# Feed-forward of a hybrid encoder block: token block sums taken from turned tiles, and half of their low parts moved to POOL

## The reference, cut to what matters

```
        h = rms_norm(x, norm_ffn_pre[l])
        gate, up = jnp.split(h @ ffn_w_gu[l], 2, axis=-1)
        f = (jax.nn.silu(gate) * up) @ ffn_w_down[l]
        x = x + rms_norm(f, norm_ffn_post[l])
```

## Time and profile before

| what | us |
|---|---|
| median of 3 runs | 1398.59 (1397.63 to 1400.22) |
| the profiled execution | 1398.22 |
| its span | 1396.1 |
| PE busy | 1373.2 (98%) |
| DVE, ACT, POOL busy | 883.2, 669.1, 876.7 |

### The profile page before, as it was taken

How to read it: one execution, slowest core, us unless ns; L and a number is a source line. 1 busy time by engine, 2 the same in 40 slices (tenths; PEclk the granted TensorE clock), 3 DMA queues, 4 the chain that set the end, 5 groups by cost and what they waited for, 6 DMA issues and landing times.

```text
span 1396.1 us, 18962 instructions
## 1 busy us (share of the span) xinstructions
PE 1373.2 (98%) x6708; PEld 1142.7 (82%) x6708; DVE 883.2 (63%) x1262; ACT 669.1 (48%) x1357; POOL 876.7 (63%) x604
## 2 busy tenths in 40 slices
PE   8999999999999999999999999999999999999998
PEld 7998888756988888888888888888888888888886
DVE  5799997887987788764277533333333333484868
ACT  6432233666686774354374533333333333544454
POOL 1697256422778976512354687777777774799653
PEclk9999999999999999999999999999999999999999
DMA  5676133440028554301535132333332324933364
GB/s 203 210 248 210 46 91 105 152 151 1 1 61 282 188 190 148 101 28 39 188 118 187 58 109 98 111 113 114 98 108 99 111 83 166 364 110 96 112 206 154
DMA packets 137757, 183.58 MB, mean 131 GB/s; under 512 B 10304, under 2 KB 82368, under 8 KB 137664
## 3 DMA queue, kind: packets, MB, share of 16 engines
q1 hardware_dynamic: 135360, 177.25, 38.8%
q10 hardware_dynamic: 2304, 5.13, 1.1%
HBM read 136.98 MB, written 45.35 MB: 131 GB/s over the span
## 4 chain that ended last, share of the span: by engine, by line
PE 78%; POOL 7%; DVE 6%; ACT 3%; issue 3%; DMA 3%; SPq 0%; DVEq 0%; POOLq 0%; ACTq 0%
PE ps L1368 23%; PE ps L1369 23%; PE ps L1370 23%; PE ps L1359 4%; PE ps L1882 2%; PE ps L1542 1%; POOL wd L1329 1%; PE ps L1580 1%; POOL w_lo L1231 1%; DMA gain_b<-f_rows 1%; PE ps L1634 1%; POOL right_b L1320 1%; DVE x L3774 1%; POOL right_a L1320 1%; POOL ws L1277 1%
## 5 line engine op out<-in xcount | busy, mean ns | idle before, releaser
L1368 PE MATMUL ps<-w_hi,t_hi 128*128 128x512 f32 (+2 forms) x576 | 219.5, 381 | 2.5 <-DVE t_lo L2990 0.7
L1370 PE MATMUL ps<-w_hi,t_lo 128*128 128x512 f32 (+2 forms) x576 | 217.5, 378 | 0.0
L1369 PE MATMUL ps<-w_lo,t_hi 128*128 128x512 f32 (+2 forms) x576 | 217.5, 378 | 0.0
L1123 POOL TENSOR_TENSOR w_lo<-raw,w_hi 128x512 fp32r<-128x512 f32 (+1 forms) x52 | 82.1, 1585 | 96.5 <-ACT w_hi L2161 96.3
L1368 PEld LDWEIGHTS ps<-w_hi,t_hi 128*128 128x128 f32 x576 | 108.2, 188 | 21.9 <-issue 1.7
L1370 PEld LDWEIGHTS ps<-w_hi,t_lo 128*128 128x128 f32 x576 | 108.2, 188 | 17.6
L1369 PEld LDWEIGHTS ps<-w_lo,t_hi 128*128 128x128 f32 x576 | 108.2, 188 | 16.9
L1247 POOL TENSOR_TENSOR w_lo<-raw,w_hi 128x512 fp32r<-128x512 f32 x32 | 41.9, 1314 | 98.3 <-ACT w_hi L2638 98.2
L3667 DVE TENSOR_TENSOR ev<-ps,ev 128x512 f32<-128x512 f32 x21 | 14.5, 692 | 138.2 <-PE ps L1370 138.2
L2161 ACT ACTIVATE w_hi<-raw 128x512 fp32r<-128x512 f32 (+1 forms) x52 | 31.4, 615 | 96.5 <-PE ps L1370 96.1
L2837 ACT ACTIVATE ev<-ps 128x512 f32<-128x512 f32 x63 | 37.5, 595 | 83.7 <-PE ps L1370 83.7
(11 more groups left out here) (390 smaller groups left out, 4144.4 us busy)
## 6 DMA issues: line engine op xcount, KB each, us to landing
raw_a<-in_ffn_w_gu_dram SPq DMA_DIRECT2D x44, 256.0 KB, 3.2
raw_b<-in_ffn_w_gu_dram SPq DMA_DIRECT2D x44, 256.0 KB, 3.2
f_rows<-fs SPq DMA_DIRECT2D x44, 256.0 KB, 3.8
gain_b<-f_rows SPq DMA_DIRECT2D x39, 256.0 KB, 2.7
tables<-f_rows SPq DMA_DIRECT2D x38, 256.0 KB, 2.7
f_rows<-fa SPq DMA_DIRECT2D x33, 256.0 KB, 3.4
raw<-in_xa_wo_dram SPq DMA_DIRECT2D x32, 256.0 KB, 2.6
wd_rest<-in_ffn_w_down_dram SPq DMA_DIRECT2D x15, 512.0 KB, 6.3
```

The costliest lines, as they stand in the source:

```text
L1123: nc.gpsimd.tensor_tensor(w_lo[:, k, 0:width], raw[:, k, 0:width], w_hi[:, k, 0:width].bitcast(F32), ALU.subtract).then_inc(w_split, 1)
L1368: nc.tensor.matmul(out, a_hi, b_hi, start=start, stop=False, skip_group_check=onto)
L1369: nc.tensor.matmul(out, a_hi, b_lo, start=False, stop=False, skip_group_check=onto)
L1370: return nc.tensor.matmul(out, a_lo, b_hi, start=False, stop=stop, skip_group_check=onto)
```

## The change

The token sums are now formed from tiles that have been turned already, and no sum is turned.

- `row_high(t)` for t < 4 copies each bank raw into `y[:, t, ...]` (the turned tile, kept in fp32) ahead of its high part: eight more ACT copies of 128x512. `xo_round(31)` now stands ahead of `row_high(3)`.
- `sum_rows_12(m)` reads the turned tile 4+m straight from its PSUM bank, so PE turns tiles 6 and 7 only when `sum_rows_12(0)` and `(1)` have let go of their banks. PE turns one tile after each of the products 0 to 3 of chunk 0.
- `third_sums(p)` and `fourth_sums(p)` (both DVE) do two tiles each, 128x1024. POOL's four `fourth_rows` are gone.
- `sum_high(n)` and the low parts do two tiles at once: 8 of 128x1024 in place of 16 of 128x512. Low parts 0 to 3 (first and second sum) are on DVE, low parts 4 to 7 (third and fourth) on POOL (`late_sum_low`).
- The weights of chunk 1 are split in the order `SUMS_AHEAD` (2, 3, 4, 5, 0, 1, 6), and two `weight_sum_of(2, n)` come between the late low parts.

```diff
 def row_high(t):
                     act.wait_ge(h_turned, 2 * t + half + 1)
+                    if t < 4:
+                        nc.scalar.activation(y[:, t, half * 512:(half + 1) * 512], bank(4 + 2 * (t % 2) + half),
+                                             ACT.Copy).then_inc(h_raw, 1)
...
 def turn_rows_h3(t):
+                    if t >= 6:
+                        pe.wait_ge(t_rows, 2 * (t - 6) + half + 1)
...
 def sum_high(n):
+                if n < 2:
+                    act.wait_ge(t_rows, 4 * n + 4)
...
+                if n == 2:
+                    act.wait_ge(g_prod, 6)
                 elif n == 4:
-                    act.wait_ge(g_prod, 6)
-                elif n == 8:
-                    act.wait_ge(t_rows, 12)
-                    act.wait_ge(t_rows4, 4)
-                act.wait_ge(t_turned, T_TURNED + n + 1)
-                nc.scalar.activation(sum_home(n)[0], four(6 + n % 2), ACT.Copy).then_inc(t_high, 1)
+                    act.wait_ge(t_rows, 10)
+                    act.wait_ge(t_rows4, 2)
+                    act.wait_ge(t_low, 4)
+                elif n == 6:
+                    act.wait_ge(t_low, 6)
+                nc.scalar.activation(sum_home(n)[0], turned_sums(n), ACT.Copy).then_inc(t_high, 1)
...
 # POOL
-            fourth_rows(0) ... fourth_rows(3)
+            for j in SUMS_AHEAD:
                 weight_low(1, j)
+            def late_sum_low(n):
+
+                pool.wait_ge(t_high, T_HIGH + n + 1)
+                high, low = sum_home(n)
+                nc.gpsimd.tensor_tensor(low, turned_sums(n), high.bitcast(F32), ALU.subtract).then_inc(t_low, 1)
+
+            late_sum_low(4)
+            late_sum_low(5)
+            late_sum_low(6)
+            weight_sum_of(2, 1)
+            late_sum_low(7)
+            weight_sum_of(2, 2)
...
 # PE
-            for n in range(3):
+            for n in range(4):
                 first_chunk(n)
                 turn_rows_h3(4 + n)
...
-            for j in range(6):
-                turn_sums((4 + 2 * j, 5 + 2 * j))
-                block_product(1, j)
...
 # ACT, from row_high(5) on
+            first_silu(0)
+            row_high(6)
+            weight_high(1, 2)
+            weight_high(1, 3)
+            row_high(7)
+            sum_high(0)
+            weight_high(1, 4)
+            weight_high(1, 5)
+            sum_high(1)
+            weight_high(1, 0)
+            sum_high(2)
+            sum_high(3)
+            weight_high(1, 1)
+            weight_high(1, 6)
+            first_silu(1)
+            bank_copy(1, 1)
+            weight_high(2, 0)
+            sum_high(4)
+            sum_high(5)
...
 # DVE
             row_low(4)
+            sum_rows_12(0)
             row_low(5)
+            sum_rows_12(1)
             row_low(6)
             row_low(7)
+            sum_rows_12(2)
+            sum_rows_12(3)
...
             first_gated(0)
             sum_low(0)
             sum_low(1)
-            sum_rows_3(0)
-            sum_rows_3(1)
+            third_sums(0)
+            third_sums(1)
             sum_low(2)
+            fourth_sums(0)
             sum_low(3)
+            fourth_sums(1)
             first_gated(1)
```

More of the change, by code:

```diff
@@ L92, in c_weights, with c_weight @@
     return 4 + PROD * (c - 1) + n if c else n
+SUMS_AHEAD = (2, 3, 4, 5, 0, 1, 6)
+def c_weight(c, j):
+    return c_weights(c, (SUMS_AHEAD.index(j) if c == 1 else j) + 1)
 def c_sums(c, n=0):
@@ L691, in sum_rows, with turned_sums @@
             kind, m = n // 4, n % 4
-            return (y[:, 4 + m, 512:1024], y[:, 4 + m, 0:512], y[:, m, 0:512], t_sum[:, m, :])[kind]
+            return (y[:, 4 + m, 512:1024], y[:, 4 + m, 0:512])[kind]
         def sum_home(n):
-            kind, m = n // 4, n % 4
+            kind, m = n // 2, n % 2 * 2
             high, low = tok_sums[(2, 1, 3, 4)[kind]]
-            c = slice(m * P, (m + 1) * P)
-            return high[:, :, c], low[:, :, c]
+            c = slice(m * P, (m + 2) * P)
+            return tuple(v[:, :, c].rearrange("p k (m i) -> p m k i", m=2) for v in (high, low))
+        def turned_sums(n):
+            kind, m = n // 2, n % 2 * 2
+            v = (y[:, 4 + m:6 + m, 512:1024], y[:, 4 + m:6 + m, 0:512], y[:, m:m + 2, 0:512], t_sum[:, m:m + 2, :])[kind]
+            return v.rearrange("p m (k i) -> p m k i", k=4)
         def memory_slots(n):
@@ L1294, in _ @@
                 weight_sum_of(1, n)
[L1295 to L1300, removed]
-                weight_low(1, j)
+            for j in SUMS_AHEAD:
+                weight_low(1, j)
+            def late_sum_low(n):
[8 more added lines that the diff above has]
+            weight_sum_of(2, 2)
             for c in range(2, NC):
                 weight_low(c, 0)
-                weight_sum_of(c, 1)
+                if c > 2:
+                    weight_sum_of(c, 1)
                 weight_low(c, 1)
-                weight_sum_of(c, 2)
+                if c > 2:
+                    weight_sum_of(c, 2)
                 weight_low(c, 2)
@@ L1990, in first_chunk @@
                 last.then_inc(g_prod, 1)
[L1992 to L2006, removed]
             def block_product(c, j):
@@ L2032, in block_product @@
                 last.then_inc(g_prod, 1)
-            for n in range(3):
+            for n in range(4):
                 first_chunk(n)
                 turn_rows_h3(4 + n)
-            turn_rows_h3(7)
-            first_chunk(3)
             first_chunk(4)
[L2040 to L2044, removed]
-            for j in range(6):
-                turn_sums((4 + 2 * j, 5 + 2 * j))
-                block_product(1, j)
-            block_product(1, 6)
-            for c in range(2, NC):
+            for n in range(5, 8):
+                first_chunk(n)
+            for c in range(1, NC):
                 for j in range(PROD):
@@ L2785, in _ @@
             row_high(2)
-            for n in range(26, 31):
+            for n in range(26, 32):
                 xo_round(n)
             row_high(3)
-            xo_round(31)
             for t in range(4, NT):
@@ L2807, in _ @@
             row_high(5)
[L2809 to L2829, removed]
             def bank_copy(c, n):
@@ L2837, in bank_copy, with first_silu @@
                 nc.scalar.activation(dst, bank(3 * (c % 2) + src_bank), ACT.Copy).then_inc(c_act, 1)
+            def first_silu(n):
+                act.wait_ge(g_prod, (2, 7)[n])
+                nc.scalar.activation(gate[:, n, :], bank(2 * n), ACT.Silu).then_inc(c_act, 1)
+            first_silu(0)
[17 more added lines that the diff above has]
+            sum_high(5)
             def gate_silu(c, n):
@@ L2844, in _ @@
             for c in range(1, NC - 1):
[L2845 to L2849, removed]
+                if c > 1:
+                    bank_copy(c, 1)
+                    weight_high(c + 1, 0)
                 weight_high(c + 1, 1)
@@ L2852, in _ @@
                 if c == 1:
-                    sum_high(12)
-                    sum_high(13)
+                    sum_high(6)
+                    sum_high(7)
                 if c > 1:
```

69 lines of the change are left out of this document (31 added, 38 removed).

## The result

Before 1398.91 us (median of 10 runs, 1397.49 to 1400.22), after 1402.74 (10 runs, 1400.55 to 1405.22): ratio 1.0028, 95% interval 1.0019 to 1.0037. The change costs 3.8 us. The profiled execution took 1403.47, its span is 1401.3.

What follows compares the result with a forecast made beforehand. PE bounds the kernel, already held by ACT and POOL at (2, 5). Gains of 7.0 + 0.4 less losses of 0.5, 1.2, 0.6, 0.2, 1.3, 4.6 and about 2.0 net +3.0: median 1401.6 us, range 1397.6 to 1404.2.

Steps and rivals of the forecast that it cites:

- What PE saves: Eight pairs of `turn_sums` leave PE at 0.88 us each, 7.0; with 0.44 for the old wait at (2, 5), some 7.5.
- Step 1: Raw copies while tiles 0 to 3 are turned delay POOL's low parts; PE loses 0.5 us, bounds 0 and 1.0.
- Step 2: Turning tiles 6 and 7: no wait at tile 6; PE waits 1.2 us for the low part of tile 7.
- Step 3: DVE's list to the fourth token sum: three meetings with POOL cost 3.1 us, so it is done at 779.0.
- Step 4: POOL's list, late low parts at 2.36 us: chunk 2's fourth weight sum ends at 802.95, 3.0 late.
- Step 5: PE waits 0.6, 0.2 and 1.3 us in chunk 1, 4.6 at (2, 2); (2, 5) starts 3.0 later.
- about 2.0, the last to (2, 5): PE loses about 2.0 us at (2, 5), waiting for `bank_copy(2, 4)`.
- rival D: The 4.6 us pause at (2, 2) lowers PE's clock; time within C's 1403 to 1405; chance no more than 0.03.
- All is shifted by the same from there: Behind (2, 5) POOL gains on PE in each chunk as before, and everything is later by the same 3.0 us.
- A, faster: Rival: gain holds if chunk 2's fourth weight sum ends before 799.96 less POOL's catch-up; 3.6 us faster, 1395.0; chance 0.10.
- B: As a rival: a tie, some 1399, if DVE loses nothing to POOL or step 1 is hidden; chance 0.27.
- C: Rival: low parts take up to 3.4 us or DVE loses 1.3 per POOL operation; 1403 to 1405; chance 0.13.

Runs made afterwards that it cites:

- e3: Changed kernel with 38 transposes of the identity added on PE ahead of its wait at (2, 2); median 1402.29 us, ratio 1.003 to the kernel before.
- e7: Kernel before, with none of the change, `weight_low(2, 0)` done three times on POOL; median 1401.26 us, ratio 1.0018 to the kernel before.
- e4: Changed kernel with late low parts 4 and 5 on DVE, 6 and 7 on POOL behind two weight sums; median 1399.42 us, ratio 1.0006 to the kernel before.
- e2: Changed kernel with `gate_silu(1, 1)` and `bank_copy(2, 1)` ahead of `weight_high(2, 4)` and `(2, 5)` on ACT; 1403.36 us, ratio 1.0034 to the kernel before.
- e8: Changed kernel with POOL waiting for the fourth token sum ahead of `weight_low(1, 1)`; measured once, 1402.19 us.
- e5: Changed kernel with all late low parts on DVE and product 3 of chunk 0 cut around tile 7's turn; 1394.82 us, ratio 0.9967 to the kernel before.

## Why the prediction was right

Forecast 1401.6 with +3.0; measured 1402.74, +3.8 in the medians, inside the range of 1397.6 to 1404.2 and slower by 0.28%. By its own steps:

- **What PE saves.** 7.0 for eight pairs isn't seen alone, but the account closes with it: with the old wait, 0.6 by starts, it is 7.6; less what PE lost by its starts (0.5 in step 1, then 1.2, 0.5, 0.3, 1.3, 4.65 and 2.9, all below) that is -3.8, and (2, 5) starts 4.51 later than in the earlier trace rows, 3.8 with the later start of this profile taken off (709.83 against 709.13).
- **Step 1.** Predicted 0.5; from the turn of tile 0 to that of tile 4 40.52 in place of 40.00.
- **Step 2.** Tile 6: no wait predicted and none found; the 0.2 for `t_lo` in the list of waits stands at the turn of tile 2, at 717.43, and was there before too (716.73). Tile 7: 1.2 predicted; from its turn at 761.19 to product 4 at 763.20 are 2.01, where 0.79 pass from the turn of tile 6 to its product, so 1.2 found.
- **Step 3.** The fourth token sum at 779.0; at 779.36, in a trace that is 0.7 late by then. Three DVE operations took 1.1 more than their 1.2, 3.3 in all where 3.1 was taken: one of the two of 3.46, and those of 2.30 and 2.31. POOL's 1.30 became 2.3 in two of these three meetings. The Trainium skill ("SBUF — State Buffer", "Who interferes with whom") calls the shared ports an exclusive lock. The trace agrees, and shows why the price is 1.1 and not the 1.3 that POOL's operation takes alone: the one that comes later waits for what is left of the other. At 772.55 POOL had 1.23 to go and DVE lost 1.1; at 773.74 DVE had 1.11 to go and POOL lost 1.0; at 774.78 POOL had 1.23 to go and DVE lost 1.1.
- **Step 4.** The fourth weight sum at 802.95; at 803.35, that is 2.7 late and not 3.0 with the later start taken off. The operation not in the trace, the late low part, took 2.37 to 2.39 (4.76 for two): the value taken, 2.36, and not the 3.4 of the upper bound.
- **Step 5.** Predicted 0.6, 0.2, 1.3 and 4.6 at (1, 4), (1, 5), (1, 6) and (2, 2). By starts (to the matmul ahead, less one step of 0.23) 0.50, 0.27, 1.29 and 4.65. The row's own figure for a wait is 0.16 less, since it counts from the end of the matmul ahead (0.39 after its start), while the next would have started 0.23 after it.
- **The term that was mis-sized, and its mechanism wrong,** is the last: "about 2.0, the last to (2, 5)", as a wait. PE never waited there. It ran 14 steps in 6.11 us (805.68 to 811.79) where 3.2 would do, 2.9 lost, and came to (2, 5) at 816.82, when the bank copy of 814.90 had been done for 1.3. With the clock kept full (e3) the term is sound: PE waits 1.8 there by starts. So rival D, given 0.03, was what happened at that place. The 0.9 between 2.9 and 2.0 is why (2, 5) comes 3.8 later and not 3.0. D's argument, "PE stood 5.17 us at the start and its clock was still granted in full", was a wrong reading: the twelve transposes behind that pause took 2.82 us, where sixteen took 1.91 in the earlier trace rows and 38 of the same identity 4.31 in e3, so PE ran there at about half speed. The views print a full clock for that stretch, but the trace holds no clock record ahead of 9.71 us. That the medians say 3.8 too is in part luck, since B adds 0.8 in the profile.
- **All is shifted by the same from there.** Nearly: B is 0.8 longer, where e7, with POOL as late, has none of it (561.84). In it stands a wait of 1.50 in the down projection, in the row below this list, where the earlier trace rows have 0.5 for POOL. No releaser is named for it, but POOL's `right_b` ends at 1245.42. Further back ACT stands 2.22 at 1209.94 for the load of a left part (`gain_b` from `f_rows`), where the seven loads ahead of it cost 0.86 to 1.48. The other kernels made from the changed one have 1.0 to 1.4 at that place of PE (e4 0.35 and 0.47), e7 0.16 and 0.44. What makes the load late in them wasn't tried and stays open.
- **The rivals.** A, faster: shown to be reachable, but not with the late low parts on POOL. "If it ends before 799.96" was the right place: with that sum at 794.86 the kernel is 5.0 faster by the medians, at 800.05 it is even, at 803.35 slower. B and C: DVE's three meetings came as counted, so neither.

The wait in the down projection, from PE's timeline of the changed kernel:

```profile
1245.52 0.47 PE L1387 MATMUL ps<-right_b,left_b 128*128 128x512 f32 x1 [1.50 <-issue]
```

## What to carry to other kernels

Work taken off the bounding engine is worth only what its suppliers can follow. Before counting the gain, look for the place where that engine already waits a little, and follow its releaser back: the 0.44 us at (2, 5) told more than the 7 us saved.

Where an operation goes to another engine, ask what is behind it in that list and who waits for the last item, and when its own input can be there: four operations on POOL cost 7.2 us of its list, two placed behind a late input still 4.7, and the same four on DVE a wait of 0.15 of PE at (1, 4).

An interval on the bounding engine's timeline ranks kernels well: A lay within a microsecond of what the medians said in each comparison made here.

## What the runs showed of the hardware

PE's granted clock fell to half, 1.2 GHz, with pauses inside a busy stretch: 4.49 us in the changed kernel, 4.17 in e2, 4.39 in e8 and 3.27 in e4 (granted clock 0.72 over 800 to 806 us). It was back in full some 6 us after the restart in the changed kernel and in e2, and 3.3 us after it in e4. It stayed full behind waits of 1.65 (e3), 1.63 (e7), 1.46 (e8) and 1.24 (e2). But a pause of 2.04 was enough once, in e5's execution, far ahead of the change:

```profile
444.82 0.47 PE L1383 MATMUL ps<-w_hi,t_hi 128*128 128x512 f32 x1 [2.04 <-DVE y L3323]
```
```profile
445.30:448.80 3.50, 3.50 (x10) 2.71 (x10) 3.45 (x4) 3.36 (x8) 3.50 (x3) 0.51 0.85 235
```

At the program's start, behind 5.17 us without work, PE ran at about half speed by the durations of its transposes, whatever the views print for the clock. The Trainium skill ("TensorE: Matmul & The Clock Gate", "HAM oscillation — how this bites in real kernels") describes a PE that waits for its data between groups of matmuls, finds its clock lowered and starts the next group slow; the trace agrees, with the 0.43 us steps above.

A pause of the bounding engine is thus paid twice, by its length and by what follows, unless the next wait swallows the second part, as it did in the changed kernel for two thirds (2.9 us lost, 0.9 of them seen at (2, 5)) and did not in e2, where 3.0 us stayed.
